# Forty tokens instead of thirty-two by fetched expert rows in a fused two-block kernel

## The chip, the cores and the metric

The kernel runs on one core of one Trainium2 chip. The metric is the device time of one execution in microseconds (us), as a median of several executions.

## The reference

Two transformer blocks are applied to 256 tokens of width 1024. What matters here is the last layer, a product-key expert layer: each token picks 16 of 16384 experts for each of 8 heads, so 128 of them, and adds up their v rows, weighted by a gate and by the gelu of the token's product with their u rows.

```python
def chunk(xc):                                   # xc: 128 tokens, normed
    q = (xc @ w_query).reshape(PEER_TOKEN_CHUNK, PEER_HEADS, 2, PEER_HALF)
    s1 = jnp.einsum('thd,hnd->thn', q[:, :, 0], sub_keys_1).astype(jnp.float32)
    s2 = jnp.einsum('thd,hnd->thn', q[:, :, 1], sub_keys_2).astype(jnp.float32)
    ...                                          # top 16 of each, then the top 16 of their sums: idx, best
    g = jax.nn.softmax(best, axis=-1)
    u = expert_u[idx]
    act = jax.nn.gelu(jnp.einsum('td,thkd->thk', xc, u).astype(jnp.float32), approximate=False)
    w = (g * act).astype(h.dtype)
    return jnp.einsum('thk,thkd->td', w, expert_v[idx])
```

The result is x plus this, normed and scaled by a last gain.

## The kernel before

The program is written by engine: each engine's instructions stand in the order in which it runs them, and semaphores tie them together. Up to 627 us of the profile it computes the first block, attention and the queries; the change leaves that alone. The expert layer then treats the tokens in two ways.

**Dense tokens.** NT = 224 tokens are multiplied with all experts. PE works through 64 products with u (`expert_in(q)`, each of 256 experts) and then 64 with v (`expert_out(q)`), each 48 matmuls of [128x128] by [128xNT] in f16: 16 pairs of output and step of the contraction, times three, since f32 weights and inputs are split in a high and a low half (`three`, L680, L683, L686). Per product SP loads 1 MB into the ring (L3268), ACT makes the high half (`expert_hi`, L2904) and DVE the low half (`expert_lo`, L2159) two products ahead. ACT's gelu takes the products with u out of PSUM into `answers` (L2935, L2932). In parallel DVE and POOL search for the best experts: DVE's turns 0 to 29 hold one step of the search each (`chosen`, L2174 to L2263). When the experts of a half of the tokens are known, PE turns their numbers and gates (`slots(t)`, L1314, L1316) after product SLOTS_AFTER[t] = 11 or 29, and DVE takes them out of the bank (`slots_evicted(t)`, L2271 to L2276) in its turns 19 and 30. From product 31 on come the gates, 8 tokens a group, 28 groups: DVE writes one-hots (L2295, L2298, L2300), PE multiplies them between its matmuls (`gates(g)`, L1331), DVE weighs the answers (`weigh`, L2309) and, for products later than a group, `weigh_late` (L2323). For the products with v, ACT casts a high half of the weighed answers (`w_hi`, L2959) and DVE subtracts it for the low one (`w_lo`, L2327). There are two pairs of these halves.

PSUM has 8 banks of 2 KB a partition. `take` gives them out in a fixed circle: a bank comes round after eight takes, and PE then waits until its last use was emptied.

**Fetched tokens.** NG = 32 tokens are computed by fetching just their experts' rows. Token p % 32 lies on partition p, NK = 4 times, and fetch n brings 128 rows of 4 KB, one for each partition (L3223, an indirect DMA issued by POOL): 32 fetches of u rows and 32 of v rows. DVE multiplies a fetched u tile with `h_rows` and sums it (`row_in`, L2336), ACT takes the gelu of all these at once (ROW_GELU), and DVE adds gate times v row into `row_sums` (`row_out`, L2351, L2354). At the end PE adds the four parts of each token (L1390) into the banks of the result. Three tiles hold the fetches; fetch n waits until row n-3 was used, and all but the first wait until product 63 with u is done, as their tiles hold weight halves before. The tables ROWS_IN and ROWS_OUT say how many rows are done by DVE's turn n (turn 64 + q belongs to product q with v): rows in at 5 for each 4 turns from turn 64 on, rows out one a turn from 91.

`h_rows` and the tables of places and gates are copied four times, by small DMAs of POOL (L3201, L3207, L3208). At product 40 with v SP reloads x and the last gain (L3256 to L3259).

Of the kernel before, what the change touches and what calls it, by code (L numbers as in the profile page):

```python
# [31 lines left out]
NG = 32  # L32
NT = S - NG
NK = 128 // NG
# [7 lines left out]
SLOTS_AFTER = (11, 29)  # L42
# [202 lines left out]
def memory(nc):  # L245
# [157 lines left out]
    def f16(ap, *shape):  # L403
# [5 lines left out]
        if len(shape) == 4:  # L409
# [13 lines left out]
                  for x_ in (t[:, 32768:33280], small[:, 512:1024]))  # L423
    m.slot_numbers = f16(small[:, 512:768], 128, 2, 2)
# [9 lines left out]
    g = Arena(t, 128 * NT, 32768)  # L434
# [5 lines left out]
    m.row_gate, m.row_dots, m.row_sel = (g.take(NG) for _ in range(3))  # L440
    a = Arena(t, 16384, 128 * NT)
# [213 lines left out]
def tensor_program(k):  # L655
# [691 lines left out]
    def expert_out(q, banks):  # L1347
# [30 lines left out]
    for i in range(4):  # L1378
# [4 lines left out]
        if i == 0:  # L1383
# [3 lines left out]
            pe.wait_ge(s["row_sel"], 1)  # L1387
# [9 lines left out]
def vector_program(k):  # L1397
# [1054 lines left out]
def scalar_program(k):  # L2452
# [983 lines left out]
```

## Time and profile before

| | |
|---|---|
| median of 3 runs | 1282.47 us (1280.68 to 1283.19) |
| the profiled execution | 1282.63 us |
| its span, first to last instruction | 1281.2 us |
| busy PE, DVE, ACT, POOL | 1220.8, 1037.7, 679.3, 313.0 us |
| mean granted PE clock | 0.991 |
| DMA, whole span | 266.44 MB, 208 GB/s |

An engine's busy time is a mean over stages that differ; which of them sets the time has to be read stage by stage. PE's matmuls overlap in the rows (each is shown with 0.26 us where a new one starts every 0.1 us), so the pace is taken from distances, not from the durations of single matmuls.

### The profile page before, as it was taken

How to read it: one execution, taken by the hardware profiler on the slowest of the kernel's cores; microseconds unless marked ns; L12 is line 12 of the kernel's file. 1: busy time of each engine (PE TensorE's matmuls, PEld its weight loads, DVE VectorE, ACT ScalarE, POOL GpSimd, SP SyncE). 2: the span in 40 equal slices, each digit the busy share in tenths (PEclk: the TensorE clock that was granted, in tenths of full speed). 3: DMA queues.
4: the chain of work that ended last, by engine and by line, in shares of the span. 5: the costliest groups of instructions: out<-in, count | busy, mean ns of one | idle time of the engine just before them, and what ended most of it. 6: DMA issues, size and time to landing. Idle time of an engine off the chain costs nothing.

```text
span 1281.2 us, 26843 instructions
## 1 busy us (share of the span) xinstructions
PE 1220.8 (95%) x11398; PEld 1031.1 (80%) x11398; DVE 1037.7 (81%) x1612; ACT 679.3 (53%) x969; POOL 313.0 (24%) x202
## 2 busy tenths in 40 slices
PE   6899888999999999999999899999999999999997
PEld 5545774888844546648999799999999989999996
DVE  4865884899956766677899789999998888989884
ACT  5663231767635435646545456776665444545553
POOL 0322221144500000000113500000004556555640
PEclk9999998999999999999999899999999999999999
DMA  7530003755566332457536656555459999999981
GB/s 292 201 107 26 2 2 132 288 206 198 205 223 250 107 103 95 139 190 259 203 132 232 214 198 219 182 194 198 171 193 336 341 337 357 358 339 402 338 315 34
DMA packets 51352, 266.44 MB, mean 208 GB/s; under 512 B 5136, under 2 KB 5408, under 8 KB 32544
## 3 DMA queue, kind: packets, MB, share of 16 engines
q1 hardware_dynamic: 40192, 226.76, 49.5%
q0 software_dynamic: 10160, 35.96, 7.5%
q10 hardware_dynamic: 880, 1.99, 0.5%
q8 instruction: 91, 1.49, 0.5%
q14 instruction: 29, 0.24, 0.1%
HBM read 262.04 MB, written 2.10 MB: 206 GB/s over the span
## 4 chain that ended last, share of the span: by engine, by line
PE 62%; DVE 22%; issue 6%; DMA 5%; ACT 4%; ACTq 0%; DVEq 0%; POOL 0%; POOLq 0%
PE bank L680 18%; PE bank L686 18%; PE bank L683 18%; DMA arena<-in_expert_rows,arena 5%; PE bank L1109 2%; DVE ring L2159 2%; DVE ring L2295 2%; DVE X L2159 2%; DVE arena L2336 1%; PE bank L760 1%; DVE arena L2309 1%; DVE arena L2159 1%; DVE ring L1793 1%; DVE arena L2298 1%; DVE HT L2159 1%
## 5 line engine op out<-in xcount | busy, mean ns | idle before, releaser
L680 PE MATMUL bank<-arena 128*128 128x256 f16 (+3 forms) x720 | 216.4, 307 | 0.6 <-DVE arena L1463 0.4
L683 PE MATMUL bank<-arena 128*128 128x256 f16 (+3 forms) x720 | 216.3, 307 | 0.0
L686 PE MATMUL bank<-arena 128*128 128x256 f16 (+3 forms) x720 | 216.2, 307 | 0.0
L1463 DVE SCALAR_TENSOR_TENSOR arena<-ring,arena 128x2048 f16<-128x2048 f32 (+1 forms) x59 | 133.9, 2273 | 31.8 <-ACT arena L2511 31.7
L3223 POOL DMA_INDIRECT arena<-in_expert_rows,arena x32 | 72.7, 2272 | 285.5 <-PE bank L686 236.2
L680 PE MATMUL bank<-cst,arena 128*128 128x224 f16 (+2 forms) x544 | 133.3, 254 | 0.4 <-DVE arena L1463 0.4
L686 PE MATMUL bank<-cst,arena 128*128 128x224 f16 (+2 forms) x544 | 133.3, 254 | 0.0
L683 PE MATMUL bank<-cst,arena 128*128 128x224 f16 (+2 forms) x544 | 133.3, 254 | 0.0
L2511 ACT ACTIVATE arena<-ring 128x2048 f16<-128x2048 f32 (+1 forms) x59 | 111.2, 1892 | 28.9 <-PE bank L686 28.9
L2959 ACT CAST arena<-arena 128x448 f16<-128x448 f32 x64 | 36.0, 565 | 138.3 <-PE bank L686 138.3
L2159 DVE SCALAR_TENSOR_TENSOR X<-ring,X 128x2048 f16<-128x2048 f32 x42 | 96.2, 2290 | 14.2 <-ACT X L2904 14.1
L3223 POOL DMA_INDIRECT arena<-in_expert_v,arena x32 | 87.9, 2748 | 61.0 <-DVE arena L2354 52.1
L2159 DVE SCALAR_TENSOR_TENSOR ring<-ring 128x2048 f16<-128x2048 f32 x42 | 96.2, 2290 | 5.5 <-ACT ring L2904 5.5
L686 PEld LDWEIGHTS bank<-arena 128*128 128x128 f16 x720 | 70.6, 98 | 36.8 <-issue 0.8
L680 PEld LDWEIGHTS bank<-arena 128*128 128x128 f16 x720 | 70.5, 98 | 36.7 <-issue 2.0
L683 PEld LDWEIGHTS bank<-arena 128*128 128x128 f16 x720 | 70.6, 98 | 34.8 <-issue 1.4
L680 PE MATMUL bank<-arena,X 128*128 128x224 f16 x352 | 91.2, 259 | 2.1 <-DVE small L2327 2.1
L3036 POOL TENSOR_TENSOR small<-small,cst 128x1 f32<-128x1 f32 (+3 forms) x16 | 18.9, 1178 | 300.1 <-DVE small L1417 300.1
L686 PE MATMUL bank<-arena,X 128*128 128x224 f16 x352 | 91.2, 259 | 0.0
L683 PE MATMUL bank<-small,X 128*128 128x224 f16 x352 | 91.2, 259 | 0.0
L680 PE MATMUL bank<-arena,HT 128*128 128x224 f16 x336 | 87.0, 259 | 2.6 <-DVE small L2327 2.5
L680 PE MATMUL bank<-cst,X 128*128 128x224 f16 x320 | 83.6, 261 | 6.1 <-DVE small L2276 6.1
(379 smaller groups left out, 3660.8 us busy)
## 6 DMA issues: line engine op xcount, KB each, us to landing
ring<-in_expert_u SPq DMA_DIRECT2D x64, 1024.0 KB, 4.8
ring<-in_expert_v SPq DMA_DIRECT2D x64, 1024.0 KB, 8.5
ring<-in_w_in_n SPq DMA_DIRECT2D x24, 1024.0 KB, 4.8
ring<-in_w_up_t SPq DMA_DIRECT2D x22, 1024.0 KB, 4.8
ring<-in_w_down_n SPq DMA_DIRECT2D x11, 1024.0 KB, 4.8
ring<-in_w_out_n SPq DMA_DIRECT2D x8, 1024.0 KB, 4.8
ring<-in_w_query_t SPq DMA_DIRECT2D x8, 1024.0 KB, 4.8
ring<-in_w_in_t SPq DMA_DIRECT2D x3, 1024.0 KB, 7.0
```

Of the source, the lines that this page charges most:

```text
L680: pe.matmul(out_, stat[0], mov[0], start=start, stop=False, skip_group_check=shared)
L683: pe.matmul(out_, stat[0], mov[1], start=False, stop=False, skip_group_check=shared)
L686: return pe.matmul(out_, stat[1], mov[0], start=False, stop=stop, skip_group_check=shared)
L760: tr = pe.transpose(b[0:rows, i * 128:(i + 1) * 128], src, ident)
L1109: mm = pe.matmul(b[:, :], m.MT[:, 4 * half + c, t * 128:(t + 1) * 128], piece[:, c, :], start=(half == 0 and c == 0), stop=(half == 1 and ...
L1463: nv.scalar_tensor_tensor(out=lo, in0=ld.slot(i), scalar=W_UP, in1=hi, op0=ALU.mult, op1=ALU.subtract).then_inc(s["split_lo"], 1)
L2159: nv.scalar_tensor_tensor(out=m.halves_l[kk], in0=ld.slot(i), scalar=W_UP, in1=m.halves_h[kk], op0=ALU.mult, op1=ALU.subtract).then_inc(s[ ...
L2295: c = step(nv.tensor_tensor(oh.rearrange("p b k a n -> p (b k) a n"), m.iota2.unsqueeze(1).broadcast_to(shape), numbers.unsqueeze(2).broad ...
L2511: na.activation(hi, ld.slot(i), ACT.Copy, scale=W_UP).then_inc(s["split_hi"], 1)
L2959: na.copy(m.Wh[n % 2][:, :, 0:NT], m.answers[:, 2 * n:2 * n + 2, :]).then_inc(s["w_hi"], 1)
L3036: ng.tensor_tensor(ap, ap, K(m, "half")[:, 0:n], ALU.pow).then_inc(s["rstd"], 1)
L3223: ng.indirect_dma_start(out=m.fetched[n % 3], out_offset=None, in_=k.d["expert_rows" if n < NG else "expert_v"], in_offset=bass.IndirectOf ...
```

## The change

- NG becomes 40 and NT 216. The fetched tokens form two groups: 32 tokens four times on the partitions with 32 fetches, and 8 tokens sixteen times with 8 fetches. There are 40 fetches of u rows and 40 of v rows, two tiles of `h_rows`, two of selection, and two products for each half of the result in the tail.
- FETCHED_IN = 10: the first ten fetches use one tile alone, which is free of weight halves, and their rows are done by DVE in turns 45, 47 to 63. From then on the three tiles go round as before, fetch n waiting for the last row of its tile. Rows in go on at 10 for each 9 turns to turn 90, rows out at 10 for each 9 turns from 91.
- The gain's load and the multiplication of `h_rows` stand behind slots 1 on POOL, as the tile lies where the search keeps its results.
- SLOTS_AFTER goes from (11, 29) to (14, 29).
- A third pair of halves for the products with v: `w_hi` runs three products ahead.
- Gate groups: 27, of 8 tokens, over the same products.

```diff
-NG = 32
+FETCHED_IN = 10
+ROW_GROUPS = (32, 8)
+NG = sum(ROW_GROUPS)
+ROW_FIRST = [sum(ROW_GROUPS[:a]) for a in range(len(ROW_GROUPS))]
...
-SLOTS_AFTER = (11, 29)
+SLOTS_AFTER = (14, 29)
...
-ROWS_IN = [max(0, min(NG, 5 * (n - 63) // 4)) for n in range(128)]
-ROWS_OUT = [max(0, min(NG, n - 90)) for n in range(128)]
+ROWS_IN = [max(0, min(NG, (n - 43) // 2 if n < 64 else 10 + 10 * (n - 63) // 9)) for n in range(128)]
+ROWS_OUT = [max(0, min(NG, 10 * (n - 90) // 9)) for n in range(128)]
...
+    m.Wh, m.Wl = (w_ + [f16(t[:, at:at + 256], 2, 256)] for w_, at in ((m.Wh, 33280), (m.Wl, 33536)))
...
-    m.h_rows = g.take(1024)
+    m.h_rows = [t[:, at:at + 1024] for at in (28672, 31744)]
-    m.fetched = [g.take(1024) for _ in range(3)][::-1]
+    m.fetched = [t[:, at:at + 1024] for at in (27648, 29696, 30720)]
...
             for hf in range(2):
-                pe.matmul(ps.tile("fin", 1, hf)[128 - NG:128, :], m.row_sel, m.row_sums[:, hf * 512:(hf + 1) * 512],
-                          start=True, stop=True)
+                for a, sel in enumerate(m.row_sel):
+                    pe.matmul(ps.tile("fin", 1, hf)[:, :], sel, m.row_sums[a][:, hf * 512:(hf + 1) * 512],
+                              start=(a == 0), stop=(a == len(m.row_sel) - 1))
...
     def w_hi(n):
-        if n >= 2:
-            na.wait_ge(s["v_done"], n - 1)
-        na.copy(m.Wh[n % 2][:, :, 0:NT], m.answers[:, 2 * n:2 * n + 2, :]).then_inc(s["w_hi"], 1)
+        if n >= 3:
+            na.wait_ge(s["v_done"], n - 2)
+        na.copy(m.Wh[n % 3][:, :, 0:NT], m.answers[:, 2 * n:2 * n + 2, :]).then_inc(s["w_hi"], 1)
...
-    for i in range(NK):
-        ng.dma_start(m.h_rows[i * NG:(i + 1) * NG, :], m.xs[3][0:NG, 0, :]).then_inc(s["rows_placed"], 16)
-    ng.dma_start(m.fetched[0], k.d["ffn_g"]).then_inc(s["row_gain_landed"], 16)
+    for h_, n, first in zip(m.h_rows, ROW_GROUPS, ROW_FIRST):
+        for i in range(128 // n):
+            ng.dma_start(h_[i * n:(i + 1) * n, :], m.xs[3][first:first + n, 0, :]).then_inc(s["rows_placed"], 16)
...
+    ng.wait_ge(*ps.free("slots", 1))
+    ng.dma_start(m.fetched[0], k.d["ffn_g"]).then_inc(s["row_gain_landed"], 16)
...
-        if n >= 3:
-            ng.wait_ge(s["rows_used"], n - 2)
+        if nth > 1:
+            ng.wait_ge(s["rows_used"], max(j for j in range(n) if k.fetch(j)[0] == kk) + 1)
...
+    def fetch(n):
+
+        of = [0] * FETCHED_IN + [i % 3 for i in range(2 * NG)]
+        return of[n], of[:n + 1].count(of[n])
```

The written order shows three places. PE, products 11 to 22 with u, before (L1314 turns the slots; `slots_named` says that the search of a half is done, `bankN_emptied` that a bank is free):

```order
L680 MATMUL bank2<-cst,ring 128x224 [waits expert_lo,bank2_emptied]
...
L1314 MATMUL bank1<-cst,arena 128x128 [waits slots_named,bank1_emptied]
L1315 MATMUL bank1<-cst,arena 128x128
L1316 MATMUL bank1<-cst,arena 128x128
L680 MATMUL bank5<-cst,arena 128x224 [waits expert_lo,bank5_emptied]
...
L680 MATMUL bank2<-cst,arena 128x224 [waits expert_lo,bank2_emptied]
...
L680 MATMUL bank1<-cst,X 128x224 [waits expert_lo,bank1_emptied]
...
L680 MATMUL bank4<-cst,X 128x224 [waits expert_lo,bank4_emptied]
```

With the change:

```order
L684 MATMUL bank2<-cst,ring 128x216 [waits expert_lo,bank2_emptied]
...
L684 MATMUL bank1<-cst,arena 128x216 [waits expert_lo,bank1_emptied]
...
L1318 MATMUL bank4<-cst,arena 128x128 [waits slots_named,bank4_emptied]
L1319 MATMUL bank4<-cst,arena 128x128
L1320 MATMUL bank4<-cst,arena 128x128
L684 MATMUL bank6<-cst,arena 128x216 [waits expert_lo,bank6_emptied]
...
L684 MATMUL bank1<-cst,X 128x216 [waits expert_lo,bank1_emptied]
...
L684 MATMUL bank4<-cst,X 128x216 [waits expert_lo,bank4_emptied]
```

The slots move from behind product 11, bank1, to behind product 14, bank4. The next taker of that bank was product 19 and is product 22.

DVE, turn 45 and the start of turn 46, before (L2295 to L2300 are one-hots, L2159 a low half, two L2309 weigh one group, L2323 a late product):

```order
L2295 TENSOR_TENSOR ring<-cst,small 128x2048 [waits bank6_filled,bank4_emptied]
L2298 TENSOR_TENSOR arena<-ring,small 128x1024 [waits vector_step]
L2300 TENSOR_TENSOR ring<-ring,small 128x2x256 [waits one_hots_eq]
L2159 SCALAR_TENSOR_TENSOR ring<-ring 128x2048 [waits expert_hi]
L2309 SCALAR_TENSOR_TENSOR arena<-bank,arena 128x88x4 [waits bank4_emptied,bank2_emptied]
L2309 SCALAR_TENSOR_TENSOR arena<-bank,arena 128x88x4 [waits bank6_emptied]
L2323 TENSOR_TENSOR arena<-arena,cst 128x2x104 [waits bank6_emptied,bank4_emptied,late]
L2295 TENSOR_TENSOR ring<-cst,small 128x2048 [waits bank2_filled,bank4_emptied]
L2298 TENSOR_TENSOR arena<-ring,small 128x1024 [waits vector_step]
```

With the change, whose lines stand 5 lower:

```order
L2300 TENSOR_TENSOR ring<-cst,small 128x2048 [waits bank5_filled,bank4_emptied]
L2303 TENSOR_TENSOR arena<-ring,small 128x1024 [waits vector_step]
L2305 TENSOR_TENSOR ring<-ring,small 128x2x256 [waits one_hots_eq]
L2164 SCALAR_TENSOR_TENSOR ring<-ring 128x2048 [waits expert_hi]
L2314 SCALAR_TENSOR_TENSOR arena<-bank,arena 128x88x4 [waits bank4_emptied,bank2_emptied]
L2314 SCALAR_TENSOR_TENSOR arena<-bank,arena 128x88x4 [waits bank6_emptied]
L2328 TENSOR_TENSOR arena<-arena,cst 128x2x104 [waits bank6_emptied,bank4_emptied,late]
L2344 ISA arena<-arena 128x1024 [waits h_rows,fetched0_landed]
L2344 ISA arena 128x1
L2300 TENSOR_TENSOR ring<-cst,small 128x2048 [waits bank6_filled,bank4_emptied]
L2303 TENSOR_TENSOR arena<-ring,small 128x1024 [waits vector_step]
L2305 TENSOR_TENSOR ring<-ring,small 128x2x256 [waits one_hots_eq]
```

Turn 45 ends with the first row in (the two ISA rows). Nine more such pairs stand in turns 47 to 63.

POOL, from the last candidates to the fetches, before (bank0_filled is product 63 with u):

```order
L3195 TENSOR_TENSOR arena<-arena 128x80 [waits halves_chosen]
L3195 TENSOR_TENSOR arena<-arena 128x22
L3215 TENSOR_TENSOR arena<-arena 128x256 [waits row_gain_landed,rows_placed]
L3215 TENSOR_TENSOR arena<-arena 128x256 x3
L3223 DMA arena<-in_expert_rows,arena 128x1024 [waits h_rows]
L3223 DMA arena<-in_expert_rows,arena 128x1024 [waits bank0_filled]
L3223 DMA arena<-in_expert_rows,arena 128x1024
L3223 DMA arena<-in_expert_rows,arena 128x1024 [waits rows_used] x29
L3223 DMA arena<-in_expert_v,arena 128x1024 [waits rows_used] x32
```

With the change:

```order
L3212 TENSOR_TENSOR arena<-arena 128x80 [waits halves_chosen]
L3212 TENSOR_TENSOR arena<-arena 128x22
L3232 DMA arena<-in_ffn_g 128x1024 [waits bank4_emptied,rows_placed]
L3237 TENSOR_TENSOR arena<-arena 128x256 [waits row_gain_landed]
L3237 TENSOR_TENSOR arena<-arena 128x256 x7
L3246 DMA arena<-in_expert_rows,arena 128x1024 [waits h_rows]
L3246 DMA arena<-in_expert_rows,arena 128x1024 [waits rows_used] x10
L3246 DMA arena<-in_expert_rows,arena 128x1024 [waits bank4_filled] x2
L3246 DMA arena<-in_expert_rows,arena 128x1024 [waits rows_used] x27
L3246 DMA arena<-in_expert_v,arena 128x1024 [waits rows_used] x40
```

The gain's load comes behind the slots' bank; eleven fetches stand ahead of the wait for product 63 instead of one.

## Rows read from the trace of the kernel before

**Rows 1.** The page, DMA rate of the span in 40 slices of 32 us.

```profile
GB/s 292 201 107 26 2 2 132 288 206 198 205 223 250 107 103 95 139 190 259 203 132 232 214 198 219 182 194 198 171 193 336 341 337 357 358 339 402 338 315 34
```

**Rows 2.** Windows: length, busy us (instructions) by engine, granted clock, DMA share, GB/s.

```profile
core 0: us, PE busy (x) PEld busy (x) DVE busy (x) ACT busy (x) POOL busy (x), PEclk, DMA share, GB/s
635.00:722.00 87.00, 87.00 (x910) 86.99 (x909) 84.10 (x302) 42.95 (x39) 26.84 (x37) 1.00 0.52 183
722.00:729.00 7.00, 0.92 (x8) 0.56 (x6) 6.33 (x22) 2.34 (x2) 4.93 (x7) 0.69 0.57 171
...
834.00:961.00 127.00, 125.04 (x1426) 123.92 (x1424) 122.84 (x144) 84.22 (x186) 0.00 (x0) 1.00 0.53 187
968.00:1097.00 129.00, 124.00 (x1284) 122.68 (x1285) 109.60 (x119) 63.60 (x54) 75.89 (x33) 1.00 0.94 345
1097.00:1149.00 52.00, 52.00 (x545) 52.00 (x544) 46.87 (x38) 26.30 (x24) 30.67 (x12) 1.00 0.98 343
1157.00:1173.00 16.00, 16.00 (x169) 16.00 (x168) 16.00 (x13) 9.43 (x9) 10.58 (x4) 1.00 1.02 406
```

**Rows 3.** ACT, timeline: start, us, line, tiles, idle before; gelus of products 17 to 19.

```profile
717.77 0.54 ACT L2935 ACTIVATE arena<-bank 128x448 f32<-128x448 f32 x1 [2.26 <-PE bank L686]
...
722.38 0.54 ACT L2935 ACTIVATE arena<-bank 128x448 f32<-128x448 f32 x1 [2.26 <-PE bank L686]
...
734.72 0.54 ACT L2935 ACTIVATE arena<-bank 128x448 f32<-128x448 f32 x1 [10.00 <-PE bank L686]
```

**Rows 4.** PE, timeline, first matmul of product 19.

```profile
728.42 0.37 PE L680 MATMUL bank<-cst,X 128*128 128x224 f16 x1 [6.08 <-DVE small L2276]
```

**Rows 5.** DVE, timeline, gates stage: a gap, and one whole turn.

```profile
833.90 2.29 DVE L2159 SCALAR_TENSOR_TENSOR ring<-ring 128x2048 f16<-128x2048 f32 x1 [1.66 <-ACT ring L2904]
...
883.07 1.22 DVE L2295 TENSOR_TENSOR ring<-cst,small 128x2048 f16<-128x2048 f16 x1
...
885.39 2.29 DVE L2159 SCALAR_TENSOR_TENSOR ring<-ring 128x2048 f16<-128x2048 f32 x1
887.59 1.00 DVE L2309 SCALAR_TENSOR_TENSOR arena<-bank,arena 128x376 f32<-128x376 f32 x2
888.72 0.43 DVE L2323 TENSOR_TENSOR arena<-arena,small 128x256 f32<-128x256 f32 x1
```

**Rows 6.** PE, timeline, its longest wait in the v stage.

```profile
1035.32 0.26 PE L680 MATMUL bank<-arena,HT 128*128 128x224 f16 x1 [1.98 <-DVE small L2327]
```

**Rows 7.** Windows of 32 us, columns as in rows 2: 256 columns, then 224.

```profile
256.00:288.00 32.00, 32.00 (x295) 28.69 (x294) 31.23 (x48) 19.82 (x28) 16.18 (x7) 1.00 0.59 210
...
1185.00:1217.00 32.00, 32.00 (x337) 32.00 (x335) 28.54 (x22) 16.64 (x14) 19.57 (x8) 1.00 0.95 338
```

**Rows 8.** POOL, timeline, the first small DMA of the places.

```profile
687.08 0.51 POOL L3207 DMA_DIRECT2D arena<-arena  x1 [36.48 <-DVE arena L2263]
```

**Rows 9.** DVE, timeline, one row in, and what follows its accumulator.

```profile
974.20 1.22 DVE L2336 CUSTOM_DVE_ANT_0 arena<-arena 128x1024 f32<-128x1024 f32 x1
...
975.47 2.29 DVE L2159 SCALAR_TENSOR_TENSOR X<-ring,X 128x2048 f16<-128x2048 f32 x1
```

**Rows 10.** POOL, landing times of row fetches, 990 to 1090 and 1157 to 1173.

```profile
DMA to landing us min/median/max: 7.7/9.7/10.7
...
DMA to landing us min/median/max: 9.4/9.8/10.1
```

**Rows 11.** DVE, timeline of the v stage: a full turn, and a wait ahead of L2327.

```profile
1158.49 2.29 DVE L2159 SCALAR_TENSOR_TENSOR HT<-ring,HT 128x2048 f16<-128x2048 f32 x1
...
1162.42 2.29 DVE L2159 SCALAR_TENSOR_TENSOR X<-ring,X 128x2048 f16<-128x2048 f32 x1
...
1241.56 0.63 DVE L2327 TENSOR_TENSOR small<-arena 128x448 f16<-128x448 f32 x1 [0.49 <-ACT arena L2959]
```

**Rows 12.** ACT, wait for a load after the reload; PE, tail, 1260 to 1264.

```profile
1152.61 1.91 ACT L2904 ACTIVATE ring<-ring 128x2048 f16<-128x2048 f32 x1 [3.08 <-DMA ring<-in_expert_v]
...
1261.97 1.90 PE L1390 MATMUL bank<-arena 128*32 128x512 f32 x4
```

More of the change, by code:

```diff
@@ L433, in memory @@
     m.oh = [f16(lent[:, 1024 * k:1024 * (k + 1)], 4, 2, 128, 2) for k in range(2)]
[L434 to L435 removed]
+    m.h_rows = [t[:, at:at + 1024] for at in (28672, 31744)]
     m.row_sums = m.h_rows
[L437 removed]
+    m.fetched = [t[:, at:at + 1024] for at in (27648, 29696, 30720)]
+    assert 128 * NT <= 27648
     g = Arena(t, 33792, END)
     m.row_at = g.take(NG).bitcast(U32)
[L440 to L441 removed]
+    m.row_gate, m.row_dots = (g.take(NG) for _ in range(2))
+    m.row_sel = [late[0][:, 128 * i:128 * (i + 1)] for i in range(len(ROW_GROUPS))]
+    a = Arena(t, 16384, 28672)
     m.qq = a.take(16, 256)
@@ L2345, in row_out @@
         n = NG + r
-        kk = n % 3
-        nv.wait_ge(s[f"fetched{kk}_landed"], 16 * (n // 3 + 1))
+        kk, nth = k.fetch(n)
+        sums = m.row_sums[row_group(r)]
+        nv.wait_ge(s[f"fetched{kk}_landed"], 16 * nth)
         if r == 0:
@@ L2924, in gelu @@
         if q == min(LATE, 14336 // (2 * NT)):
-            na.wait_ge(s["rows_placed"], 16 * 3 * NK)
+            na.wait_ge(s["rows_placed"], 16 * 3 * sum(128 // n for n in ROW_GROUPS))
         src = ps.tile("u", q)[:, :].rearrange("p (j n) -> p j n", j=2)
@@ L3210, in gpsimd_program @@
+    for n, first in zip(ROW_GROUPS, ROW_FIRST):
+        of, to = slice(first, first + n), slice(first, first + n)
+        for i in range(128 // n):
+            rows, at = slice(i * n, (i + 1) * n), slice(i * n, (i + 1) * n)
+            ng.dma_start(m.row_at[rows, to], m.places[of, at]).then_inc(s["rows_placed"], 16)
+            ng.dma_start(m.row_gate[rows, to], gate[of, at]).then_inc(s["rows_placed"], 16)
     choose(1)
-    ng.wait_ge(s["rows_placed"], 16 * 3 * NK)
+    ng.wait_ge(s["rows_placed"], 16 * 3 * sum(128 // n for n in ROW_GROUPS))
@@ L3212, in gpsimd_program @@
+    ng.wait_ge(*ps.free("slots", 1))
+    ng.dma_start(m.fetched[0], k.d["ffn_g"]).then_inc(s["row_gain_landed"], 16)
     ng.wait_ge(s["row_gain_landed"], 16)
-    for i in range(4):
-        at = slice(i * 256, (i + 1) * 256)
-        ng.tensor_tensor(m.h_rows[:, at], m.h_rows[:, at], m.fetched[0][:, at], ALU.mult).then_inc(s["h_rows"], 1)
+    for h_ in m.h_rows:
+        for i in range(4):
+            at = slice(i * 256, (i + 1) * 256)
+            ng.tensor_tensor(h_[:, at], h_[:, at], m.fetched[0][:, at], ALU.mult).then_inc(s["h_rows"], 1)
@@ L3223, in gpsimd_program @@
         ng.indirect_dma_start(
-            out=m.fetched[n % 3], out_offset=None, in_=k.d["expert_rows" if n < NG else "expert_v"],
+            out=m.fetched[kk], out_offset=None, in_=k.d["expert_rows" if n < NG else "expert_v"],
             in_offset=bass.IndirectOffsetOnAxis(ap=m.row_at[:, n % NG:n % NG + 1], axis=0),
-        ).then_inc(s[f"fetched{n % 3}_landed"], 16)
+        ).then_inc(s[f"fetched{kk}_landed"], 16)
     for t in range(2):
```

53 lines of the change are left out of this document (30 added, 23 removed).

## The prediction

> **What bounds the kernel now.** The change acts from 627 us on. I read a table of windows first, to see in each stage whether PE (TensorE) is full, and then timelines of the engine that PE waits for. In the windows [rows 2] the reader should look at PE, DVE and the DMA share:
> - Products with u, 0 to 29 (635 to 782 us): PE is full except in 722 to 729, where it is busy 0.92 of 7 us. One product takes 4.60 us, the distance of two gelus, 717.77 to 722.38 [rows 3]. The next gelu is at 734.72, 12.34 later, so product 19 costs 7.74 extra. Of these PE stands for 6.08, waiting for DVE's eviction of the first turned slots [rows 4]; the rest goes at a lower granted clock, 0.69 over 722 to 729 [rows 2], a mix of its levels of 1.2 and 2.4 GHz, after the standstill.
> - Gates, products 30 to 63 (783 to 961): in 834 to 961 PE is busy 125.04 of 127 us and DVE 122.84 of its own [rows 2]. DVE's turn there is 2.32 for one-hots (883.07 to 885.39), 2.20 for a low half, 1.13 for a weighing, 0.3 for a late one: 5.96 us, growing [rows 5]. Its only gap of length is 1.66 us at 833.9 [rows 5]. The end of this stage is held by both.
> - Products with v (968 to 1260): PE is busy 124 of 129 us up to 1097 and full after [rows 2]. The longest of its waits is 1.98 us, for the low half of the weights [rows 6], which stands on DVE behind a row that had not landed. DMA moves 345 GB/s there at a share of 0.94, and 343 at 0.98 after it [rows 2].
>
> **Width.** The window at 256 columns counts 295 matmuls in 32 us, the one at 224 counts 337 [rows 7]: 108.5 and 95.0 ns, 0.42 ns a column. Eight columns fewer give 3.4 ns, times 48 matmuls 0.16 us a product: 4.60 becomes 4.44.
>
> **The sum, part by part.**
> 1. *Products 0 to 28*: 29 x 0.16 = **-4.7**. DVE is the risk: it is busy 84.1 of 87 us [rows 2], 97%, and the products become 3.5% shorter. It has a lead of about one product; I take nothing, with +1 as the bound.
> 2. *Slots turned after 14*: a bank comes round after eight takes. The one of the slots is wanted by product 19, and DVE empties it in its turn 19, behind a low half that waits for PE's product 18: so PE waits for DVE and DVE for PE. Turned after 14, the bank is wanted by product 22, three products (13 us) later than DVE's turn: **-7.7**. That PE reaches the slots later costs nothing, since they are named by 687.08 [rows 8] and product 14 ends near 700.
> 3. *Small transfers on POOL*: 20 instead of 4 for the copied rows, 40 instead of 8 for places and gates, 0.5 us each [rows 8]: 8 and 16 us more of POOL. The first lot runs until some 638 and is covered by the search, which reads POOL's candidates only from 650; the second until some 707, with eight candidate steps behind it that DVE begins to read at its turn 20, near 723. Cost 0; if both covers fail, 5 at most. Gain, multiplications and first fetch now begin near 770 and end before 795; the first row is wanted 15 turns after 770, near 858. ACT's wait for the placed rows at product 31 is met long before.
> 4. *DVE in the gates stage*. It becomes the bound alone, since PE's product falls by 0.16 and DVE's turn does not. It begins 12.4 earlier (1 and 2). A row in is 1.27 us (974.20 to 975.47 [rows 9]); nine of the ten lie before the first product with v can start, **+11.4**. One group of gates less: 2.32 for the one-hots and 1.1 for the weighing [rows 5], **-3.4**; the late weighing is a little narrower, by estimate **-0.5**; DVE's gap of 1.66 and some 0.3 of small ones vanish, **-2.0**. The start of the products with v, 968.2 now, moves by -12.4 + 5.5 = **-6.9**, and PE waits some 0.9 us a product. Bounds: the tenth row and nothing else hidden, -5.6; each of ten fetches through one tile late by 1 us, +3.1; DVE's gaps larger than I saw, -7.5.
> 5. *Products with v*, 62 to the tail: 62 x 0.16 = **-9.9**. Then the waits, 5.0 us (129 less 124 [rows 2]; 4.8 are waits of PE). A tile's round is a fetch of 9.7 (7.7 to 10.7 [rows 10]), 1.27 of use and 0.3 until POOL issues again; a third of that, 3.8 to 4.0 us, is what one fetch costs. The plan of before asked for one in 4.60 x 4/5 = 3.68 us; the new one asks for one in 4.44 x 9/10 = 4.00. It fits, barely. The third pair of halves takes away 0.49 us for which DVE stands in every turn [rows 11] and lets DVE be later by almost a product before PE notices. DVE's turn at full load is 3.93 us (1158.49 to 1162.42 [rows 11]), with a ninth of a second row 4.07, under 4.44. I take the waits as gone, **-4.8**, and put **+2.5** for new ones: doubled rows in every ninth turn, and the reload of x, after which ACT stands 3.08 us for a load [rows 12] while PE is just untouched.
> 6. *Tail*: four pieces for two products of selection by row sums take 1.90 us [rows 12]; there are two products more, **+1.9**. The last matmuls are narrower and the last low half is ready earlier, **-0.6**. Memsets and reductions between the stages (some 1 us of DVE) have 2 us of cover before product 2 needs its halves: 0.
>
> Sum: -6.9 - 9.9 - 4.8 + 2.5 + 1.9 - 0.6 = -17.8. The profiled execution took 1282.6 (span 1281.2), 0.1 above the median of the runs; so **1264.5 us**.
>
> **DMA, the shared resource.** Per product with v the new plan moves 1.049 MB of v and 10/9 x 0.524 MB of rows, 1.63 MB in 4.44 us = 367 GB/s, more than the 345 and 343 of now. But where the loads caught up, 1157 to 1173, it moved 406 GB/s [rows 2], and fetches still landed in 9.4 to 10.1 us [rows 10]. So I charge nothing. The Trainium skill (DMA: Bandwidth & Descriptors, "Where 436 GB/s comes from") says that transfers between HBM and SBUF are bound by HBM at about 358 GB/s a core. The trace exceeds that for 16 us; by the rule a product would take 4.56 us and the whole some 10 us more than my sum.
>
> **Rivals.**
> - *DMA tops out near 358 on average*, by the slices of now: only the one with the catch-up, 402, is above 358 [rows 1]. A product takes 1.63/0.358 = 4.56 us, +7.4 over 62; the reload of x (1.57 MB) is hidden no longer, +4.4 less the 2.5 counted: 1274. Against it: the 406.
> - *The round of three tiles decides.* If fetches take 10.8 us under more load, a third of the round is 4.13, a product 4.59: +9, 1273.5. For it: landings up to 10.7, and the waits of now are of this kind. Against: 9.4 to 10.1 at 406 GB/s.
> - *The gates stage costs more*: DVE waits for rows fetched through one tile, or loses its lead already in the search: +2 to +6, 1267 to 1271.
> - *The slots' change does not do what it says*, another bank or turn makes the same wait: +7.7, 1272. Against: the order of PE shows product 22 as the next taker.
> - *Slower.* The 345 GB/s of 968 to 1097 is all that this mix of loads and row fetches sustains. Then a product takes 4.73 us, +18 over 62, the reload +2: 1284.5, and with longer rounds of fetches 1290. It decides from 347 GB/s down. For it: the share was 0.94 to 0.98. Against: PE's waits there came from the round, and 406 was moved.
>
> **Numbers.** Forecast 0.60; DMA near 358 0.10; round 0.12; gates 0.09; slots 0.02; slower 0.07, of which 0.01 ends within 0.2% (2.6 us, what a measurement of this kernel can tell from none). The forecast's own range is 1259 to 1269, by its bounds; the others but the last end by 1275. So 1258 to 1276 leaves out less than 0.2. Faster 0.92, same 0.02, slower 0.06.
>
> **What would show it.** Gelus 4.44 us apart up to the gates, no wait of PE for slots (a gap at 22 would be wrong). From 770 to 950 DVE without gaps, ten rows in among its turns, PE waiting about 0.9 a product, first product with v near 961. In the v stage the casts of the high halves 4.44 apart, DMA near 365 GB/s. The forecast is wrong if they lie 4.55 or more apart: with ACT waiting for loads it is DMA, with DVE waiting for fetches it is the round. In the tail eight pieces instead of four.

## The result: 0.8% faster, half of what was forecast

| | before | changed |
|---|---|---|
| median of the runs, us | 1282.78 (1280.68 to 1283.20, 6 runs) | 1272.62 (1271.04 to 1274.77, 6 runs) |
| profiled execution, us (span) | 1282.63 (1281.2) | 1272.76 (1271.4) |

The ratio is 0.9924, interval 0.9912 to 0.9937: about 10 us, where the forecast was 18. 1272.62 lies in the range (1258 to 1276), 8.1 us above the forecast, but outside the forecast's own bounds (1259 to 1269).

Where the time went is read best by five marks that every kernel of this case has: POOL's first transfer of copied rows, the eviction of the second slots on DVE, the first product with v on PE, ACT's first eviction of the finished sums, and the end of the span. The marks in the timelines of the kernel before, in this order (start us, us, engine, line, operation, tiles, idle before it and its releaser):

```profile
627.43 2.01 POOL L3201 DMA_DIRECT2D arena<-arena  x4 [41.25 <-DVEq L1412]
782.77 0.42 DVE L2271 CAST small<-bank 128x256 f16<-128x256 f32 x1 [0.70 <-PE bank L1316]
968.21 0.26 PE L680 MATMUL bank<-arena,X 128*128 128x224 f16 x1 [0.79 <-DVE small L2327]
1262.08 0.53 ACT L2993 COPY arena<-bank 128x448 f32<-128x448 f32 x1 [2.15 <-PE bank L686]
```

And in those of the changed kernel:

```profile
626.75 9.92 POOL L3219 DMA_DIRECT2D arena<-arena  x20 [41.25 <-DVEq L1417]
770.18 0.42 DVE L2276 CAST small<-bank 128x256 f16<-128x256 f32 x1 [0.70 <-PE bank L1320]
963.22 0.25 PE L684 MATMUL bank<-arena,X 128*128 128x216 f16 x1 [1.52 <-DVE small L2332]
1244.63 0.52 ACT L3010 COPY arena<-bank 128x432 f32<-128x432 f32 x1 [4.30 <-PE bank L690]
```

Their distances give four stages. The forecast's column sorts the terms of its sum by the same marks.

| stage | before | changed | moved by | forecast |
|---|---|---|---|---|
| u: to the second slots | 155.34 | 143.43 | -11.91 | -12.4 |
| gates: to the first product with v | 185.44 | 193.04 | +7.60 | +5.5 |
| v: to the first eviction of the sums | 293.87 | 281.41 | -12.46 | -12.2 |
| tail: to the end | 19.12 | 26.77 | +7.65 | +1.3 |

With 0.68 us less ahead of the first mark this is -9.8, the difference of the two spans. Two stages came out within 0.5 us of the forecast. The gates cost 2.1 us more, and the tail 6.3 more. The second half of the document is about these two.

**The tail.** PE's first matmul of the selection by row sums, in the timeline of the changed kernel, and the group of its source line (duration of one in ns, min/median/max):

```profile
1248.23 5.37 PE L1395 MATMUL bank<-arena,cst 128*128 128x512 f32 x8 [3.63 <-DVE arena L2364]
```

```profile
L1395 PE MATMUL bank<-arena,cst x8: 592/824/1057, 1248.2 to 1253.0; 128*128 128x512 f32 x8
```

PE stands 3.63 us for L2364, the addition of a fetched row. Before, the selection followed its product at once [rows 12]. Then eight pieces take 5.37 us, some at 592 ns each as before, some at 1057. Windows of the changed kernel (columns as in rows 2):

```profile
1216.00:1248.00 32.00, 28.60 (x310) 28.29 (x307) 30.40 (x24) 13.84 (x12) 19.38 (x7) 1.00 0.75 263
...
1244.60:1248.20 3.60, 0.00 (x0) 0.01 (x1) 2.46 (x2) 0.52 (x1) 0.00 (x0) 1.00 0.33 125
1248.20:1253.60 5.40, 5.37 (x10) 2.27 (x11) 0.00 (x0) 0.00 (x0) 0.00 (x0) 0.68 0.00 0
```

PE does nothing for 3.6 us, and in the 5.4 us behind that the granted clock is 0.68, a mix of 1.2 and 2.4 GHz. What DVE does meanwhile stands in its timeline:

```profile
1242.58 0.60 DVE L2332 TENSOR_TENSOR small<-arena 128x432 f16<-128x432 f32 x1
1243.10 2.68 DVE L2364 SCALAR_TENSOR_TENSOR arena<-arena 128x1024 f32<-128x1024 f32 x2
1246.80 1.28 DVE L2364 SCALAR_TENSOR_TENSOR arena<-arena 128x1024 f32<-128x1024 f32 x1 [1.02 <-DMA arena<-in_expert_v,arena]
```

The last low half of the weights (L2332) is done at 1243.2, in time for PE. Behind it three rows are still to be added: the plan of the changed kernel puts row 37 into turn 125 and rows 38 and 39 into turn 126. Before, `min(NG, n - 90)` ended with turn 122. Two of the three are DVE's own order; the third also waits 1.02 us for its fetch.

**The gates stage.** DVE almost without gaps (busy 186.9 of 193 us from 770 to 963), as forecast, but around 780 its operations are longer. Its timeline there, two turns:

```profile
775.70 1.22 DVE L2300 TENSOR_TENSOR ring<-cst,small 128x2048 f16<-128x2048 f16 x1
776.95 1.10 DVE L2303 TENSOR_TENSOR arena<-ring,small 128x1024 f16<-128x1024 f16 x1
778.09 0.83 DVE L2305 TENSOR_TENSOR ring<-ring,small 128x512 f16<-128x512 f16 x1
778.85 2.81 DVE L2164 SCALAR_TENSOR_TENSOR arena<-ring,arena 128x2048 f16<-128x2048 f32 x1
781.58 1.75 DVE L2300 TENSOR_TENSOR ring<-cst,small 128x2048 f16<-128x2048 f16 x1
...
790.25 0.69 DVE L2303 TENSOR_TENSOR arena<-ring,small 128x1024 f16<-128x1024 f16 x1
790.97 0.42 DVE L2305 TENSOR_TENSOR ring<-ring,small 128x512 f16<-128x512 f16 x1
791.31 2.28 DVE L2164 SCALAR_TENSOR_TENSOR ring<-ring 128x2048 f16<-128x2048 f32 x1
```

From 776.95 to 788, seven operations take 0.41 to 0.54 us each more than the same ones at 790, 3.3 us together (1.10 for 0.69, 0.83 for 0.42, 2.81 for 2.28; 1.75 for the 1.22 at 775.70). POOL's timelines, of the changed kernel and of the one before, say what runs beside it:

```profile
776.47 12.19 POOL L3237 TENSOR_TENSOR arena<-arena 128x256 f32<-128x256 f32 x8 [4.04 <-DMA arena<-in_ffn_g]
```

```profile
727.36 2.76 POOL L3215 TENSOR_TENSOR arena<-arena 128x256 f32<-128x256 f32 x4
```

Eight multiplications of the copied rows by the gain, 1.5 us each, beside DVE's busiest turns. Before they were four of 0.7 us, while PE stood [rows 4] and DVE, from 728.4 on, as well. The Trainium skill describes this (SBUF — State Buffer, "SBUF: two separate sides"): DVE operations with two inputs in SBUF (or in a two-port mode) and GpSimd's share one pair of ports, which is given to one of them for a whole instruction. The rows agree: 0.41 to 0.54 us of delay, whatever the length of the DVE operation, is under the 0.7 us of one POOL piece alone. That these multiplications are the cause is tested in e2 and e6.

**The v stage** went as forecast. The page's DMA rate, in 40 slices as in rows 1:

```profile
GB/s 299 198 106 28 2 2 133 271 227 181 218 224 231 128 108 100 103 229 209 248 113 245 242 224 217 201 202 213 223 207 324 375 377 358 373 365 405 364 322 67
```

375, 377, 358, 373, 365, 405, 364: DMA moves what the plan asks for. Before, all full slices of this stage but one had 336 to 358 [rows 1]. DVE still stands for rows, 26.6 us in 21 waits (16.9 in 10 before), but little of it reaches PE, whose waits behind the first product fall from 5.0 to 3.1 us.

### The profile page after: what moved, and what is told of

It reads as the page before. It is cut to its first block, busy times and chain, and to the rows that moved or that the text cites. A ratio compares the mean times of both kernels' runs of the same rounds, so it can differ in the third digit from the quotient of the medians.

```text
span 1271.4 us, 26906 instructions
## 1 busy us (share of the span) xinstructions
PE 1200.5 (94%) x11386; PEld 1008.8 (79%) x11386; DVE 1050.1 (83%) x1635; ACT 675.7 (53%) x963; POOL 371.5 (29%) x270
## 4 chain that ended last, share of the span: by engine, by line
PE 45%; DVE 28%; DMA 14%; issue 8%; ACT 4%; DVEq 0%; ACTq 0%; POOL 0%; POOLq 0%
PE bank L684 12%; PE bank L690 12%; PE bank L687 12%; DMA arena<-in_expert_v,arena 8%; DMA arena<-in_expert_rows,arena 5%; DVE ring L2300 3%; DVE arena L2344 2%; PE bank L1113 2%; DVE X L2164 2%; DVE ring L2164 2%; DVE arena L2364 2%; DVE arena L2314 2%; DVE arena L2303 2%; PE bank L764 1%; DVE arena L2164 1%
## 5 line engine op out<-in xcount | busy, mean ns | idle before, releaser
L3246 POOL DMA_INDIRECT arena<-in_expert_rows,arena x40 | 93.5, 2337 | 199.4 <-DVE arena L2344 198.5
L684 PE MATMUL bank<-cst,arena 128*128 128x216 f16 (+2 forms) x544 | 132.2, 252 | 0.4 <-DVE arena L1468 0.4
L690 PE MATMUL bank<-cst,arena 128*128 128x216 f16 (+2 forms) x544 | 132.2, 252 | 0.0
L687 PE MATMUL bank<-cst,arena 128*128 128x216 f16 (+2 forms) x544 | 132.1, 252 | 0.0
L3246 POOL DMA_INDIRECT arena<-in_expert_v,arena x40 | 100.4, 2509 | 61.6 <-DVE arena L2364 52.4
L2974 ACT CAST arena<-arena 128x432 f16<-128x432 f32 x64 | 35.1, 551 | 119.8 <-PE bank L690 115.5
L684 PE MATMUL bank<-arena,X 128*128 128x216 f16 x352 | 90.1, 256 | 1.5 <-DVE small L2332 1.5
L690 PE MATMUL bank<-arena,X 128*128 128x216 f16 x352 | 90.1, 256 | 0.0
L687 PE MATMUL bank<-small,X 128*128 128x216 f16 x352 | 90.1, 256 | 0.0
L684 PE MATMUL bank<-arena,HT 128*128 128x216 f16 x336 | 86.0, 256 | 3.1 <-DVE arena L2332 3.1
L684 PE MATMUL bank<-arena,ring 128*128 128x216 f16 x336 | 86.0, 256 | 0.0
```

The costliest lines, as they stand in the source:

```text
L684: pe.matmul(out_, stat[0], mov[0], start=start, stop=False, skip_group_check=shared)
L687: pe.matmul(out_, stat[0], mov[1], start=False, stop=False, skip_group_check=shared)
L690: return pe.matmul(out_, stat[1], mov[0], start=False, stop=stop, skip_group_check=shared)
L2974: na.copy(m.Wh[n % 3][:, :, 0:NT], m.answers[:, 2 * n:2 * n + 2, :]).then_inc(s["w_hi"], 1)
L3246: ng.indirect_dma_start(out=m.fetched[kk], out_offset=None, in_=k.d["expert_rows" if n < NG else "expert_v"], in_offset=bass.IndirectOffse ...
```

## The experiments

All times beside runs of the kernel before on the same chip. The stages are read by the marks above.

**e1: the selection later in the tail.**

```diff
-        if i == 0:
+        if i == 2:
             ...
-        else:
-            kept_turned(i - 1)
+            kept_turned(0)
+            kept_turned(1)
+        elif i == 3:
+            kept_turned(2)
```

> Edit to the changed kernel: in the tail PE's four (now eight) selections by row sums stand after the last products' third quarter instead of after the first. Theory (last row): the 8 us that the prediction missed sit mostly in the tail. PE stands 3.63 us at 1248.23 for the last fetched row, whose turn is now 126 where it was 122, and the eight pieces behind that standstill take 5.37 instead of 3.8 us, because the clock fell. Two quarters later (4.4 us) the row has been added, PE does not stand, and the pieces take 3.8: 3.6 to 5.2 us faster than the changed kernel, 1267.4 to 1269.0. Rival (the end is held by what follows: evictions, the last transposes, the sum on DVE): PE's wait only moves, below 1 us faster, 1271.6 to 1272.6.

Measured: 1267.27 us, ratio 0.9876 (0.9858 to 0.9894), where the changed kernel has 0.9924. 5.35 us less, just above the upper end. The tail takes 21.23 us instead of 26.77, the other stages are unchanged (143.42, 193.14, 281.05). The group of the selection:

```profile
L1395 PE MATMUL bank<-arena,cst x8: 592/593/612, 1249.2 to 1252.2; 128*128 128x512 f32 x8
```

No wait, and no piece longer than 612 ns, in windows 3.60 us busy of 3.60 at a granted clock of 1.00. The 5.5 us of the tail are 3.63 of standing and some 1.8 of lower clock behind it. What is left of the tail, 2.1 us above before, is the four pieces more (3.62 for 1.90) and 0.4 that was not traced.

**e2: POOL's multiplications made narrow.** Most of the rows' gain is left out of the computation.

```diff
-            at = slice(i * 256, (i + 1) * 256)
+            at = slice(i * 256, i * 256 + 4)
```

> Edit: each of POOL's eight multiplications of the copied rows by the gain takes 4 columns in place of 256, so most of the rows go in without their gain (left out of the computation). Theory (two engines share their access to memory): while POOL multiplies, 776.47 to 788.66, DVE's one-hots take 1.75, 1.10 and 0.84 where they take 1.22, 0.69 and 0.42 elsewhere, and its low halves 2.81 in place of 2.28, 3.3 us in all. DVE is the bound of the gates stage, so without them the first product with v starts 3.3 us earlier, near 959.9 in place of 963.2, and the end comes 3.3 earlier, 1269.3. Rival A (PE becomes the bound of that stage as soon as DVE gains): under 1.5 us of it arrive. Rival B (the slow DVE operations have another cause, the transfer or the place in the ring): they stay as long as they are, and nothing changes.

Measured: 1270.29 us, ratio 0.9906 (0.9884 to 0.9929). The gates stage takes 190.60 instead of 193.04, so 2.4 of the 3.3 us arrive, more than rival A allowed. DVE's timeline, the third turn's one-hots:

```profile
781.88 1.21 DVE L2300 TENSOR_TENSOR ring<-cst,small 128x2048 f16<-128x2048 f16 x1
783.12 0.72 DVE L2303 TENSOR_TENSOR arena<-ring,small 128x1024 f16<-128x1024 f16 x1
```

1.21 and 0.72 where there were 1.75 and 1.10: rival B is out. The profiled execution as a whole (span 1271.3) shows less, since it reached the first mark 1.6 us later and its v stage took 282.86; the verdict rests on the stage and on the DVE rows.

**e3: the first slots after product 11 again.**

```diff
-SLOTS_AFTER = (14, 29)
+SLOTS_AFTER = (11, 29)
```

> Edit: the first slots are turned after product 11 again, all else as in the changed kernel. Theory: PE's wait for the eviction of the slots at product 19 comes back (5 to 6 us, 7.7 with the lower clock after it), and as DVE stands in the same ring of waits, it is not caught up in the gates stage: 7 to 8 us slower, 1280. Rival (the gates stage is bound by DVE, which has the slack to catch up): the wait is there but 1 to 3 us arrive at the end, 1273.6 to 1275.6.

Measured: 1281.71 us, ratio 0.9983 (0.9966 to 1.0001), 9.1 above the changed kernel. PE's timeline has the wait back, 6.32 where it was 6.08 [rows 4]:

```profile
725.34 0.36 PE L684 MATMUL bank<-cst,X 128*128 128x216 f16 x1 [6.32 <-DVE small L2281]
```

The u stage takes 151.68 us instead of 143.43, and the gates stage 193.14, the same: nothing is caught up. It is 8.3 us by the stage; the medians' other 0.8 is within what executions of this kernel differ by.

**e4: two pairs of weight halves.**

```diff
-        if n >= 3:
-            na.wait_ge(s["v_done"], n - 2)
+        if n >= 2:
+            na.wait_ge(s["v_done"], n - 1)
```

and `% 2` for `% 3` at the places of the halves; ACT casts the half of product q + 2 in turn q, not that of q + 3.

> Edit: two pairs of weight halves again (the cast of the high half waits for the product two before), all else as in the changed kernel. Theory: DVE stands 0.49 us again in each turn of the products with v; its turn with one row becomes 3.92 plus 0.49, 4.41 against a product of 4.43, and a turn with two rows 5.7: PE waits a little in each turn with two rows and at every late row, 3 to 7 us slower, 1276 to 1280. Rival 1 (the third pair does nothing): within 1 us of the changed kernel. Rival 2 (rows decide): DVE is later with every row, the round of the three tiles becomes longer, and the last row out comes later too: over 7 us slower.

Measured: 1275.13 us, ratio 0.9940 (0.9923 to 0.9957), against 0.9924: the intervals overlap. DVE does stand again, as its timeline shows,

```profile
1111.67 0.61 DVE L2332 TENSOR_TENSOR small<-arena 128x432 f16<-128x432 f32 x1 [0.34 <-ACT arena L2974]
```

but the v stage is no longer for it (280.91 us). The 3 to 7 us were wrong: between 963 and 1250 DVE stands for ACT in 17 turns, 5.6 us in all and 0.34 at most, where I had counted 0.49 in every turn. Only the tail is 1.4 us longer there (28.18), behind a wait of 3.7 for the last row. What the third pair is worth is between nothing and 2.5 us and stays open.

**e5: the slots' move alone, in the kernel before.** The same line as in e3, the other way round.

> Edit to the kernel before: the first slots turned after product 14, nothing else. Theory: PE's wait of 6.08 us at product 19 goes, with the slower clock behind it; DVE, which stood in the same ring of waits, starts the gates stage as much earlier. 6 to 7.7 us faster than before, ratio 0.9940 to 0.9953. Rival (the gates stage of before is held by DVE and the later start of the placed rows, or the wait goes to another bank): 0 to 3 us faster, ratio over 0.9976.

Measured: 1274.05 us, ratio 0.9928 (0.9914 to 0.9941). The u stage falls from 155.34 to 147.60 (-7.74, the forecast was -7.7), the gates stage stays (185.40), the v stage is 1.6 us shorter (292.29), which can be chance: one and the same v stage took 279.85 us in e12 and 282.86 in e2. The slots' move alone is 0.72% of the 0.76% that the whole change brings. Against this kernel the changed one wins 4.17 us in u by its width and 10.88 in v, and loses 7.64 in the gates stage and 7.58 in the tail: in stages the rest of the change loses 0.2 us. Eight more fetched tokens paid for themselves and no more.

**e6 and e8: rows multiplied once, before they are copied**, on top of e1.

```diff
+    ng.dma_start(h0[0:NG, :], m.xs[3][0:NG, 0, :]).then_inc(s["rows_placed"], 16)
+    ng.dma_start(gain, k.d["ffn_g"][0:NG, :]).then_inc(s["row_gain_landed"], 16)
...
+    for i in range(4):
+        at = slice(i * 256, (i + 1) * 256)
+        ng.tensor_tensor(h0[0:NG, at], h0[0:NG, at], gain[:, at], ALU.mult).then_inc(s["h_rows"], 1)
+    ng.wait_ge(s["h_rows"], 4)
+    for i in range(16):
+        ng.dma_start(h1[8 * i:8 * i + 8, :], h0[32:40, :]).then_inc(s["rows_placed"], 16)
     choose(0)
```

> Edit to e1: POOL multiplies the 40 rows by the gain once, in 4 pieces of 40 partitions right at 627 us, before it copies them; the gain lies in the place of the one-hots until then. The 8 multiplications after the slots are gone. Theory (POOL's multiplications slow DVE, and only what DVE loses after 770 counts): slots to first product with v 191.2 us as in the run with narrow multiplications, where e1 has 193.7; DVE's search takes some 1.5 us of delay from the 4 pieces near 633, of which its own waits before 770 cover a part: 1 to 2.5 us faster than e1, 1264.8 to 1266.3. Rival (POOL's small transfers after the pieces make the candidates late, DVE's search waits for them): second slots later than 770.2 by 2 to 6 us, as much slower than e1.

> The kernel of e6 again, beside that of e1 on one chip: e6's profile showed 4.4 us less than e1's, its median 0.3 less. Theory: slots to first product with v takes 191.1 us where e1 has 193.7, a fixed order of work that returns in every execution: 2 to 4 us faster than the e1 kernel of this call. Rival (the difference of the profiles was chance): below 1 us.

> The kernel of e1 again, as the measure for the two others of this call: ratio to before 0.986 to 0.989.

Measured: e6 1266.98 us, ratio 0.9882 (0.9866 to 0.9897); again, as e8, 1266.94, 0.9875 (0.9854 to 0.9897); e1's kernel again, as e9, 1268.31, 0.9892 (0.9873 to 0.9911). The gates stage takes 190.52 and 190.60 us, with e1's kernel 193.14 and 193.15: what e2 showed, now with nothing left out. POOL's pieces in the timeline of e6:

```profile
631.07 2.78 POOL L3228 TENSOR_TENSOR arena<-arena 40x256 f32<-40x256 f32 x4 [3.31 <-DMA arena<-in_ffn_g]
634.15 7.98 POOL L3231 DMA_DIRECT2D arena<-arena  x16 [0.29 <-POOL arena L3228]
```

0.7 us each, and the u stage is as long as before the edit (143.43): the candidates still come in time. But in the medians only 0.3 and 1.4 us show (for e8 I expected 2 to 4), inside the intervals, since the v stage varies by more between executions (279.98 and 281.33 here, 281.05 and 280.02 with e1's kernel). The 2.5 us are shown for the stage, for the whole they are not settled. Both versions beat the changed kernel by 4 to 6 us.

**e7: six rows beside u instead of ten**, on top of e1.

```diff
-FETCHED_IN = 10
+FETCHED_IN = 6
-... (n - 43) // 2 if n < 64 else 10 + 10 * (n - 63) // 9 ...
+... (n - 51) // 2 if n < 64 else 6 + 34 * (n - 63) // 27 ...
```

> Edit to e1: 6 instead of 10 rows come in beside the products with u; 34 instead of 30 then in 27 products with v. Theory of the prediction (one fetch costs a third of a round of some 11.4 us, 3.8 to 4.0): the gates stage is four rows of 1.14 us shorter, -4.6, the first product with v near 959.3; but the plan asks for a row in 3.52 us, the tiles give one in 3.8 to 4.0, so the rows take 129 to 136 us for 27 products that want 120, and PE is made to wait, +9 to +16: 4 to 11 us slower than e1, 1271.5 to 1278.5. Rival (fetches follow each other faster when they are wanted faster, DMA has room): no new waits, 3 to 4.6 faster than e1, 1262.7 to 1264.3.

Measured: 1278.59 us, ratio 0.9965 (0.9951 to 0.9979), 11.3 above e1's first run, at the upper end of the expectation. The gates stage is 3.94 us shorter (189.20), the v stage 14.7 longer (295.74). In the waits of 963 to 1250 DVE stands for fetched rows 22.6 us in the first part and 9.7 in the second:

```profile
DVE arena L2346 <- DMA arena<-in_expert_rows,arena: 22.6, 13, 2.7
DVE arena L2366 <- DMA arena<-in_expert_v,arena: 9.7, 8, 3.1
```

A row in 3.52 us is more than three tiles give. DMA is not at its end: it moves 341 GB/s in 964 to 1100, where e1's kernel moves 369, and a fetch lands no later (9.8 us in the median in 970 to 1080, 10.0 in the changed kernel). By these numbers it is the fetches in flight that are too few; no run with a fourth tile tests that.

**e10: the first low half of the weights sooner**, on top of e6.

```diff
+        if q == 63:
+            w_lo(0)
         if q + 2 >= EARLY and q + 2 not in WHOLE:
             expert_lo(...)
...
         if q == 63:
-            w_lo(0)
             w_lo(1)
...
     for q in range(64):
+        if q == 40:
+            selections()
```

> Edit to e6: DVE makes the first low half of the weights before the low half of the third product's values, and the matrices of the selection at turn 40 of the products with v instead of before turn 0. Theory: PE's wait of 1.5 us before the first product with v goes, and DVE, which has 1.5 us less to do before product 2, is not late there: 1.2 to 1.8 us faster than e6. Rival (the wait moves to product 2, which DVE reaches late for a row that has not landed, or to the next row): under 0.5 us faster.

Measured: 1269.24 us, ratio 0.9894 (0.9875 to 0.9913), beside e8 with 0.9875: not faster. The wait of 1.52 us before the first product with v is gone. PE's waits behind it in its timeline:

```profile
970.70 0.25 PE L685 MATMUL bank<-arena,HT 128*128 128x216 f16 x1 [0.54 <-DVE arena L2335]
976.25 0.25 PE L685 MATMUL bank<-arena,X 128*128 128x216 f16 x1 [0.95 <-DVE small L2335]
```

From the second slots to the first eviction of the sums it takes 474.46 us, e8 471.93, e6 470.50. The rival holds: PE is there earlier and waits for the low halves instead, 6.4 us in all against 4.1 in e8.

**e11 and e12: the rows out end with turn 124; the changed kernel again.**

```diff
-ROWS_OUT = [max(0, min(NG, 10 * (n - 90) // 9)) for n in range(128)]
+ROWS_OUT = [max(0, min(NG, 20 * (n - 90) // 17)) for n in range(128)]
```

> Edit to the changed kernel: the rows out are spread over turns 91 to 124 instead of 91 to 126; the selection stays where the change has it. Theory (PE stands in the tail because DVE has three rows left behind its last low half, in turns 125 and 126): the rows end two turns earlier, PE's wait of 3.6 us and the slow pieces go, -3.6 to -5.2; but the plan then asks for a row in 34/40 of 4.44 = 3.77 us, where a third of a round is 3.8 to 4.0, so DVE gets up to 0.2 us later per row, 3 to 8 us in all, of which PE feels what is over DVE's lead: +1 to +4. Together 0 to 4 us faster than the changed kernel of this call. Rival (the fetches set when the last row comes, not the turn it is planned for): the row lands as late as now, PE's wait in the tail stays over 2 us, and nothing is won, -0.5 to +3 us.

> The changed kernel again, unedited, as the measure beside e11: ratio to before 0.991 to 0.994, slots to first product with v 193.0 to 193.2 us, PE's wait in the tail 3.6 us.

Measured: e11 1276.06 us, ratio 0.9940 (0.9924 to 0.9955); e12 1272.83, 0.9918 (0.9899 to 0.9936). In e12 PE waits 3.5 us in the tail and the gates stage takes 193.05: what was read of one execution returns. In e11 the tail is 21.17 us, PE waits for no row there, and the pieces take 592 to 612 ns, as the theory had it. But the v stage grows from 279.85 to 289.18, by 9.3 where I expected 1 to 4, and instead of 0 to 4 us faster the kernel is 3.2 slower than e12 by the medians. PE's waits for one form of the low half in e11 (us in total, times, longest), then one window of e11 and of e12:

```profile
PE bank L684 <- DVE small L2332: 7.9, 6, 2.2
```

```profile
1095.00:1240.00 145.00, 138.41 (x1470) 136.34 (x1469) 127.44 (x98) 72.65 (x62) 84.88 (x36) 0.99 0.97 362
```

```profile
1095.00:1240.00 145.00, 144.65 (x1564) 144.35 (x1563) 133.10 (x102) 77.72 (x66) 79.64 (x36) 1.00 0.97 366
```

With a row asked for every 3.77 us PE is busy 138.4 of 145 us, with one every 4.00 it is 144.7. So the cause of the tail's 5.5 us is confirmed from a second side, and the cure by an earlier plan costs more than it gives.

## Why the forecast was half right

What bounds the first three stages was named rightly; two stages came out within 0.5 us and the gates within 2.1. That 1272.62 is inside the range is luck: the part above 1269 was put there for the rivals (DMA, the round, the gates, the slots), and the miss came mainly from the tail, which none of them named.

1. *Products 0 to 28, width*: forecast -4.7. The u stage of the changed kernel is 4.17 us shorter than that of e5, which has the slots' move alone. Right; the half us is DVE, for which PE now waits 2.17 us at the second slots (1.5 before).
2. *Slots*: forecast -7.7; e5 -7.74, e3 +8.3. Right, with its mechanism: PE is busy 7.00 of the 7 us from 722 to 729 now, and the granted clock there is 1.00.
3. *Small transfers on POOL*: forecast 0. Right for the transfers (the u stage came out, and did so in e6 with POOL 5 us later at the search). This is also where the step failed that follows: I asked when POOL's multiplications would be *done*, and not what they do to DVE while they run.
4. *Gates stage*: forecast +5.5, measured +7.60. The sum of DVE's own work was good: with narrow multiplications the stage is 190.60, +5.16. The failed term is one that isn't there: contention with POOL, 2.44 us. One item was off in the other direction: a row in moves DVE by 1.14 us, not 1.27, as its second instruction runs beside the next operation. Nine rows cost 1.2 us less by this, so some 0.8 of the 5.16 was not traced. PE's waits were 13.5 us in 12 pieces, nearly all after 850, and not 0.9 in each of 34 products. DVE's timeline at one row in:

```profile
919.74 1.22 DVE L2344 CUSTOM_DVE_ANT_0 arena<-arena 128x1024 f32<-128x1024 f32 x1
920.88 0.08 DVE L2344 DVE_READ_ACCUMULATOR2_ANT arena<- 128x1 f32 x1
920.88 1.22 DVE L2300 TENSOR_TENSOR ring<-cst,small 128x2048 f16<-128x2048 f16 x1
```

5. *Products with v*: forecast -12.2, measured -12.46 (-14.0 in e12). The terms hold: ACT's casts of the high halves come 4.44 us apart, and PE's waits of 5.0 us before are 3.1 now (1.5 in e12), where I had 2.5. That the sum agrees to 0.3 us is partly luck, as the same v stage differs by 3.0 us between executions. "It fits, barely" was right: asked for a row every 4.00 us, PE loses the 3.1 us at most, every 3.77 us costs some 9 us more (e11), every 3.52 us in the first part some 15 (e7). One reading was wrong: DVE did not stand 0.49 us in every turn before, but in 29 turns, 15.1 us in all. For the third pair of halves I gave the right sign at best (e4). DMA was let pass at 367 GB/s, and it passed.
6. *Tail*: forecast +1.3, measured +7.65. This is the step that failed, and most of the miss. I priced the four pieces more (1.9; they take 1.72) and never asked when the last row is added. The prediction used ROWS_OUT for its rate alone. Its end, turn 126 for 122, stands in the same line, and PE waits in the program for all rows behind the first quarter of products 62 and 63. The price is 3.63 us of standing and 1.8 of lower clock. Without it the tail is 2.1 us longer than before (e1), not 1.3: the -0.6 did not come.

The rivals: DMA near 358 GB/s, and the slower case at 345, are refuted by the rates above and by the casts 4.44 us apart; ACT stood for loads only from 1138 to 1150, behind the reload of x, 7.9 us in all and 4.4 at most. The round did not decide here: its waits are on DVE, and PE felt 3.1 us of them at most, and the last row's 1.02 in the tail; in e7 it did decide. The gates stage cost 2.1 more, the lower end of that rival, by another cause than it named. None of them named the tail.

The sum closes: 1264.5, +0.5 (u), +2.1 (gates), -0.3 (v), +6.4 (tail) and -0.7 (ahead of the first mark) give 1272.5.

## What to carry to other kernels

A schedule written as a rate has an end, and the end can cost more than the rate: where a consumer waits for the last of a series, count in which turn that last one falls and what stands behind it. When work moves to an idle engine, look for what the others do at that time with the same ports, not only whether it is done by its due time. And give a final reduction the latest place that the program allows: here two quarters of the last two products later, 4.4 us, was worth half as much as the whole change.

## What the runs showed of the hardware

- A standstill costs twice. PE stood 3.63 us, and the eight pieces behind it took 5.37 us at a granted clock of 0.68, where they take 3.62 at 1.00 (e1). The price does not go by the length of the standstill: behind 2.93 us (e2) and 3.51 us (e12) the pieces took 5.37 as well, behind 3.73 us (e4) 6.61, and there the granted clock was 0.59.
- POOL's multiplications slowed only part of DVE's work. Beside two-input operations a piece of 256 columns took 1.5 us and delayed each of them by 0.41 to 0.54. In e6 the same pieces on 40 partitions ran beside DVE's search (MAX8, FIND_INDEX8, with one input each) and took 0.7, as those on 128 partitions did before (2.76 for four), and the u stage stayed at 143.43 us.
- One input is no safeguard. DVE's cast of the slots took 0.55 us in the kernel before and 0.56 in e5, where POOL multiplied beside it. It took 0.23 in the changed kernel and at the second slots of the kernel before, where POOL did not. Before, then changed, first slots:

```profile
727.61 0.55 DVE L2275 CAST rows<-small 128x128 f32<-128x128 f16 x1
```

```profile
724.32 0.23 DVE L2280 CAST rows<-small 128x128 f32<-128x128 f16 x1
```

The Trainium skill (SBUF — State Buffer, "SBUF: two separate sides") names with the two-input operations those in a two-port mode. Two inputs and the untouched search agree with it; in which mode the cast ran no row shows.

- It goes the other way too. In the changed kernel POOL's two small additions for the search, which take 0.51 us at 640.24, take 2.47 where DVE's low half began just before them:

```profile
721.48 2.27 DVE L2164 SCALAR_TENSOR_TENSOR arena<-ring,arena 128x2048 f16<-128x2048 f32 x1
```

```profile
721.64 2.47 POOL L3212 TENSOR_TENSOR arena<-arena 128x80 f32<-128x80 f32 x2 [2.06 <-DVE arena L2191]
```

There DVE's operation is no longer than elsewhere (2.28).

- One core alone moved 405 GB/s over 32 us (the 37th slice of the changed kernel's page) and 362 over 136 us, with row fetches on POOL's queue among them, which landed in 9.8 to 10.0 us in the median. The 358 GB/s a core that the prediction weighed are no ceiling here.
